# Packing the small matmuls of an RWKV-7 recurrence into parts of the TensorE array, and starting the first two tiles from half-tile loads

## The reference, cut to what matters

```
h = rms_norm(x, norm_mix);  p = h @ w_in            # 512 x 2048 times 2048 x 9000-odd
q, k_att, v_att, rw, gate_a, gate_b = split_last(p, IN_SPLITS)
y_attn = sliding_window_attention(q, k_att, v_att, sinks)          # 16 heads of 64
def step(S, inp):                                    # RWKV-7, 16 heads of 64, 512 steps
    r_t, w_t, k_t, v_t, kk_t, a_t = inp
    sa = einsum('bhij,bhj->bhi', S, -kk_t)
    S = S * w_t + sa x (kk_t * a_t) + v_t x k_t
    return S, einsum('bhij,bhj->bhi', S, r_t)
merged = sigmoid(gate_a) * (y_attn @ w_branch_attn) + sigmoid(gate_b) * (y_rwkv @ w_branch_rwkv)
x = x + merged @ w_out
x = x + (silu(h2 @ ffn_gate) * (h2 @ ffn_up)) @ ffn_down;  out = rms_norm(x, norm_final)
```

## Time and profile before

| | |
|---|---|
| median of three runs | 3014.94 us |
| the profiled execution | 3015.46 us |
| its span, first to last instruction | 3013.4 us |
| mean granted TensorE clock | 0.994 of full speed |
| PE busy | 2949.5 us, 98% of the span, 15226 instructions |
| DVE, ACT, POOL busy | 917.6, 946.9, 1291.0 us |
| first matmul begins | 11.74 us |
| HBM traffic | 98 GB/s mean |

### The profile page before, as it was taken

How to read it: one execution, slowest core, us unless ns; L and a number is a source line. 1 busy time by engine, 2 the same in 40 slices (tenths; PEclk the granted TensorE clock), 3 DMA queues, 4 the chain that set the end, 5 groups by cost and what they waited for, 6 DMA issues and landing times.

```text
span 3013.4 us, 38711 instructions
## 1 busy us (share of the span) xinstructions
PE 2949.5 (98%) x15226; PEld 2373.1 (79%) x15226; DVE 917.6 (30%) x1380; ACT 946.9 (31%) x1213; POOL 1291.0 (43%) x1037
## 2 busy tenths in 40 slices
PE   7999999999999998999999999999999999999997
PEld 5777777777777776788888888888888888888885
DVE  5566355264363453433331110111101111011123
ACT  4354333343343343222233321233213331122221
POOL 5333324233233233555554444444445444544453
PEclk9999999999999999999999999999999999999998
DMA  4212212122122123343433222322222222322222
GB/s 160 84 71 97 77 60 101 59 78 86 54 81 90 50 97 115 133 146 140 146 139 139 97 82 98 113 97 96 83 100 98 97 97 86 109 97 97 89 88 102
DMA packets 63225, 296.12 MB, mean 98 GB/s; under 512 B 6688, under 2 KB 7968, under 8 KB 38688
## 3 DMA queue, kind: packets, MB, share of 16 engines
q1 hardware_dynamic: 55168, 280.17, 26.3%
q10 hardware_dynamic: 7968, 14.68, 1.3%
HBM read 274.12 MB, written 20.71 MB: 98 GB/s over the span
## 4 chain that ended last, share of the span: by engine, by line
PE 92%; DVE 3%; issue 2%; ACT 1%; POOL 1%; DVEq 0%; DMA 0%; POOLq 0%; SPq 0%; ACTq 0%
PE dense L1181 27%; PE dense L1183 26%; PE dense L1182 26%; PE work L1384 1%; PE work L1365 1%; PE work L1182 1%; PE work L1181 1%; PE work L1183 1%; PE work L1374 1%; DVE Y L1022 1%; PE work L1341 1%; POOL wlo L474 1%; PE work L1353 0%; PE work L1434 0%; PE work L1342 0%
## 5 line engine op out<-in xcount | busy, mean ns | idle before, releaser
L474 POOL TENSOR_TENSOR wlo<-raw,whi 128x512 fp32r<-128x512 f32 (+1 forms) x1016 | 1265.9, 1276 | 1684.8 <-ACT whi L520 1684.8
L1181 PE MATMUL dense<-H_hi,whi 128*128 128x512 f32 x2672 | 1080.1, 404 | 26.8 <-DVE wlo L806 11.7
L1183 PE MATMUL dense<-H_hi,wlo 128*128 128x512 f32 x2672 | 1044.7, 391 | 0.0
L1182 PE MATMUL dense<-H_lo,whi 128*128 128x512 f32 x2672 | 1043.5, 391 | 0.0
L520 ACT ACTIVATE whi<-raw 128x2048 fp32r<-128x2048 f32 (+1 forms) x255 | 454.6, 1783 | 1474.0 <-PE dense L1183 1394.1
L1181 PEld LDWEIGHTS dense<-H_hi,whi 128*128 128x128 f32 x2672 | 502.9, 188 | 162.5 <-issue 39.3
L1183 PEld LDWEIGHTS dense<-H_hi,wlo 128*128 128x128 f32 x2672 | 502.9, 188 | 108.4
L1182 PEld LDWEIGHTS dense<-H_lo,whi 128*128 128x128 f32 x2672 | 503.7, 189 | 101.2 <-issue 5.8
L1183 PE MATMUL dense<-G_hi,wlo 128*128 128x512 f32 x704 | 273.9, 389 | 0.0
L1181 PE MATMUL dense<-G_hi,whi 128*128 128x512 f32 x704 | 273.9, 389 | 0.0
L1182 PE MATMUL dense<-G_lo,whi 128*128 128x512 f32 x704 | 273.9, 389 | 0.0
(11 more groups left out here) (235 smaller groups left out, 2365.8 us busy)
## 6 DMA issues: line engine op xcount, KB each, us to landing
raw<-w_slots SPq DMA_DIRECT2D x103, 1024.0 KB, 4.9
raw<-w_gu SPq DMA_DIRECT2D x88, 1024.0 KB, 4.7
raw<-w_down SPq DMA_DIRECT2D x64, 704.0 KB, 4.0
gates_dram<-gout ACTq DMA_DIRECT2D x32, 256.0 KB, 2.0
gin<-gates_dram SPq DMA_DIRECT2D x16, 512.0 KB, 3.9
X<-xT SPq DMA_DIRECT2D x8, 512.0 KB, 10.5
xin<-xT SPq DMA_DIRECT2D x16, 256.0 KB, 3.5
x_dram<-x ACTq DMA_DIRECT2D x16, 256.0 KB, 3.7
```

The costliest lines, as they stand in the source:

```text
L474: done = nc.gpsimd.tensor_tensor(wlo[s][:, at], raw[s][:, at], whi[s][:, at].bitcast(f32), SUB)
L1181: PE.matmul(bank[:], whi[s][:, wk], hi[:, k, :], start=(k == first), stop=False)
L1182: PE.matmul(bank[:], whi[s][:, wk], lo[:, k, :], start=False, stop=False)
L1183: done = PE.matmul(bank[:], wlo[s][:, wk], hi[:, k, :], start=False, stop=(k == last))
```

## The change

It has two parts.

**Packing in the recurrence.** (a) The second product of each level is cut finer: for each head and block, instead of one matmul with 64 rows and 128 columns of weights on 64 moving columns, there are two with 64x64 weights on 32 moving columns, so that the four of a block lie in the four quadrants of the array (row part e, column part c). The last level has the same form now. (b) The first join writes head e to the partitions of `heads[e]`, so its matmuls alternate between column parts; its results then lie in both halves of `Lt`, ScalarE copies them in one operation of 128x256 and the transposes in two of 64x256. (c) The second join takes its weights from row part e and writes to bank `RP[e]`, so its matmuls alternate between row parts, and VectorE copies it in two operations. (d) The Gram blocks are issued as `icl` for both heads and then `kap` for both, and the wait for the banks comes once for each t.

**The start.** The first halves of weight tiles 0 and 1 are loaded right behind the first and the second X transfer, the second halves behind the fourth and the sixth. ScalarE splits the two tiles in quarters of 512 columns between the `H_hi` parts, and the squares come behind all of them; its table is loaded ahead by a small copy. VectorE does all low parts of tiles 0, 1 and 2 and the whole sum of squares. GpSimd begins with tile 3. TensorE takes four steps of tile 0, four of tile 1, and so on for two quarters, then the rest of tile 0 and the rest of tile 1; the sum over the squares comes behind tile 2. `kT` and `vT` move to memory that X held.

The diff, cut to its core:

```
@@ loads (SyncE)
             for g in range(KD // 2):
-                if g == 1:
-                    load(index(0, 2, 0))
-                    load(index(0, 2, 1))
                 sp.dma_start(X[:, 2 * g:2 * g + 2, :], ...).then_inc(x_loaded[g], 16)
+                if g < 2:
+                    sp.dma_start(raw[g][:, 0:half], w_slots[g][:, 0:half]).then_inc(first_raw[g], 16)
+                if g in (3, 5):
+                    s = (g - 3) // 2
+                    sp.dma_start(raw[s][:, half:SLOT], ...).then_inc(raw_loaded[s], 16)
@@ GpSimd
-            pool.wait_ge(lo_ready, 1)
-            low_part(index(0, 2, 1))
...
-            low_part(index(0, 2, 2))
+            pool.wait_ge(lo_ready, 3)
@@ ScalarE
+            act.wait_ge(warm, 1)
+            copy(tmp1[:, 0:1], proj[:, 0:1])
+            for q in range(4):
+                first_split(0, q)
+                for k in range(4 * q, 4 * q + 4):
+                    hi_part(k)
+                if q < 2:
+                    first_split(1, q)
+            for q in (2, 3):
+                first_split(1, q)
+            for k in range(6):
                 square(k)
+            split(index(0, 2, 2))
             act.wait_ge(tile_done, 1)
             copy(kT[0][:], dense[0][:]).then_inc(evacuated, 1)
-            split(index(0, 2, 2))
+            for k in range(6, KD):
+                square(k)
+            split(index(0, 2, 3))
@@ ScalarE, joins
-                    copy(join_w, R[4][0:CHUNK, :]).then_inc(join_w_read, 1)
+                    copy(join_w, R[4][:, 0:NB * CHUNK]).then_inc(join_w_read, 1)
-                    copy(join_x, R[3][0:CHUNK, :]).then_inc(join_x_read, 1)
+                    for e in range(2):
+                        done = copy(join_x[heads[e]], R[3][0:CHUNK, e * NB * CHUNK:(e + 1) * NB * CHUNK])
@@ TensorE, start
+            for q in range(4):
+                first_steps(0, q)
+                if q < 2:
+                    first_steps(1, q)
+            for q in (2, 3):
+                first_steps(1, q)
+            front_tile(index(0, 2, 2))
             pe.wait_ge(cst_loaded, 16)
-            for j in range(2):
-                pe.wait_ge(sq_used[j], KD // 2)
-                done = PE.matmul(R[0][:], ones, sqsum[j][:], start=(j == 0), stop=(j == 1))
+            pe.wait_ge(sq_used, KD)
+            PE.matmul(R[0][:], ones, sqsum[:], start=True, stop=True).then_inc(ss_done, 1)
@@ TensorE, Gram blocks
-                            if w >= 4:
-                                pe.wait_ge(l_read, p * (2 * NB) + w - 3)
+                        if t >= 2:
+                            pe.wait_ge(l_read, p * (2 * NB) + 2 * t - 2)
@@ TensorE, second product of a level
+                                for c in range(2):
+                                    first_col = t * HALF + c * (HALF // 2)
+                                    done = PE.matmul(RP[e][heads[c], first_col:first_col + HALF // 2],
+                                                     Xc[heads[e], t, heads[c]],
+                                                     W1[heads[e], t, c * (HALF // 2):(c + 1) * (HALF // 2)],
@@ TensorE, joins
+                            done = PE.matmul(R[4][heads[e], at], Lcross[second, e, t, :],
                                              Y[second, e, t, second], start=True, stop=True)
...
+                            done = PE.matmul(RP[e][first, at], join_x[heads[e], at],
+                                             join_w[heads[e], at], start=True, stop=True)
```

More of the change, by code:

```diff
@@ L54 @@
 DSLOT = FG * P
+QUARTER = SLOT // 4
 LOW_PIECES = 4
@@ L157, in build_layer @@
     att = Arena(nc, start.at)
+    kT = [att(f"kT{g}", [T_SEQ]) for g in range(STAGES)]
+    vT = [att(f"vT{g}", [T_SEQ]) for g in range(STAGES)]
     pT = att("pT", [2, 2, T_SEQ])
@@ L191, in build_layer @@
     Xc = Lt[:, 0]
[L192 to L193 removed]
+    join_x, join_w = (Lt[:, i].rearrange("p t n -> p (t n)")[:, 0:NB * CHUNK] for i in range(2))
     W1 = rw("W1", [NB, HALF])
@@ L236, in build_layer @@
         hi_ready, lo_ready = sem("hi_ready"), sem("lo_ready")
+        first_raw = [sem(f"first_raw{s}") for s in range(2)]
+        first_hi, first_lo, warm = sem("first_hi"), sem("first_lo"), sem("warm")
         tile_done = sem("tile_done")
@@ L558, in _ @@
             A.activation(rstd1[:], rstd1[:], ACT.Sqrt).then_inc(rms_ready, 1)
-            for n in range(1, ATT_TILES):
+            for n in range(2, ATT_TILES):
                 split(index(0, 2, n + 2))
@@ L793, in fence @@
                 V.drain()
-            V.memset(proj[:, 0:1], 0.0)
+            V.memset(proj[:, 0:1], 0.0).then_inc(warm, 1)
             dve.wait_ge(norms_loaded, 16)
[L799 to L812, removed]
+            V.memset(sqsum[:], 0.0)
@@ new lines, in _ @@
+            for q in range(4):
+                first_low(0, q)
+                for k in range(4 * q, 4 * q + 4):
+                    dve.wait_ge(h_hi_ready, k + 1)
+                    V.scalar_tensor_tensor(H_lo[:, k, :], X[:, k, :], norm_g[:, 0, k:k + 1],
+                                           H_hi[:, k, :].bitcast(f32), MUL, SUB).then_inc(h_lo_ready, 1)
+                if q < 2:
+                    first_low(1, q)
+            for q in (2, 3):
+                first_low(1, q)
+            for k in range(6):
+                add_square(k)
@@ L814, in _ @@
+            dve.wait_ge(hi_ready, 3)
+            V.tensor_tensor(wlo[0][:], raw[0][:], whi[0][:].bitcast(f32), SUB).then_inc(lo_ready, 1)
+            for k in range(6, KD):
+                add_square(k)
             dve.wait_ge(ss_done, 1)
@@ L1400, in _ @@
                     first, second = heads
[L1401 to L1404, removed]
+                    for t in range(NB):
+                        at = slice(t * CHUNK, (t + 1) * CHUNK)
+                        for e in range(2):
+                            done = PE.matmul(R[4][heads[e], at], Lcross[second, e, t, :],
                                              Y[second, e, t, second], start=True, stop=True)
```

112 lines of the change are left out of this document (54 added, 58 removed).

## The result

The changed kernel takes 2988.03 us (median of four runs, 2986.98 to 2988.91), against 3014.80 before; the ratio is 0.9911, with a 95% interval of 0.9899 to 0.9922. The forecast was 2986.5, with 2979 to 3001 around it. The profiled execution took 2988.91 us, its span is 2987.1, 26.3 less than before.

A forecast was written before the change was run, and what follows sets the result against it. The prediction took PE, busy 92%, as the bound: 13.5 us from the start plus 15.0 from eight pairs of the recurrence make 28.5, so 3015.46 becomes 2987.0, or 2986.5 by the median; range 2979 to 3001.

The forecast's parts named there:

- first matmul: At the kernel's start, PE's first matmul was to come at 8.4 us instead of waiting until 11.74.
- lost to the half-speed clock: At the start, PE running at half clock was to cost 2.0 us, within 1.4 to 3.0.
- tile 3 begins: PE was to reach weight tile 3 at 44.4 us instead of 57.9, gaining 13.5, bounds 10 and 15.
- levels, a pair: Second product in quadrants: burst 0.69 us instead of 1.11, three levels saving 0.42 and the last 0.11, 1.37 per pair.
- Gram wait, a pair: Waiting for two Gram blocks delays DVE's fifth: 0.42 us lost; a rival at 0.10 had no cost, 2983 us.
- joins, a pair: The recurrence's two joins were to shorten from 1.11 to 0.69 and 1.14 to 0.64, saving 0.42 and 0.50 us.
- all of a pair: Sum for one pair of the recurrence: 1.37 + 0.42 + 0.50 - 0.42 = 1.87 us; times 8, 15.0.
- The level that the prediction struck: Level where a gate tile ends: PE arrives 0.4 us earlier but waits for ACT, so its saving was not counted.
- From there on nothing of it is given back: After tile 3 begins, the start's 13.5 us was to be kept: a tile takes PE 11 us, GpSimd 5.
- the two-wide quadrants: Rival, chance 0.15: quadrants of the second product overlap in two rows only, a pair's levels give -0.27 us, total 2999.6.
- the slower one at 59 ns an instruction: Rival, chance 0.03: quadrant instructions don't overlap, 32 take 2.1 us instead of 1.11, total 3039 us.
- the weak start: Rival, chance 0.12: DVE or ACT falls behind, PE stutters, the clock falls; the start gains 6 to 8, total 2993.

The follow-up runs named there:

- experiment 10: Changed kernel with the second product of the levels back in its old form, all else as changed: 3000.57 us, ratio 0.9952.
- experiment 3: Changed kernel with the Gram blocks in the old order and with the old waits, one block read ahead of each: 2985.39 us, ratio 0.9904.
- experiment 1: The new start alone, with the recurrence as in the kernel before: 3004.30 us, ratio 0.9965.
- experiment 4: Changed kernel with ScalarE's sigmoid and store of a gate tile three steps into the next tile, split unmoved: 2984.19 us, ratio 0.9899.
- experiment 5: Changed kernel with GpSimd's low part of tile 14 held until VectorE has normalised one attention unit's probabilities: 2986.94 us, ratio 0.9906.
- experiment 2: The packed recurrence alone, with the start of the kernel before: 2999.83 us, ratio 0.9948.
- experiment 6: Changed kernel with a level's second product issued for all blocks of head 0, then all of head 1: 2990.82 us, ratio 0.9920.
- experiment 9: Kernel of experiment 7 with one dense step per pair moved from before the token transposes to the end of level 0: 2975.30 us, ratio 0.9868.
- experiment 7: Changed kernel with the edits of experiment 3, experiment 4 and experiment 5 together: 2979.19 us, ratio 0.9880.
- experiment 8: Kernel of experiment 7 with the second product also issued head by head, as in experiment 6: 2982.06 us, ratio 0.9893.

## Why the prediction was right

| term | forecast, us | measured, us |
|---|---|---|
| first matmul | 8.4 | 8.98 |
| lost to the half-speed clock | 2.0 | 2.6 (13 matmuls of 0.43 instead of 0.23) |
| tile 3 begins | 44.4 | 44.95; 57.9 before |
| given back in attention | 0 | 1.3 near 194; 0.8 near 218, not in every kernel |
| levels, a pair | 1.37 | 1.44 (experiment 10) |
| Gram wait, a pair | -0.42 | -0.43 (experiment 3) |
| joins, a pair | 0.92 | 0.43 + 0.46 by the bursts, in no experiment of their own |
| all of a pair | 1.87 | 1.85 (the three rows above give 1.90) |
| behind the last pair | 0 | 0.8 less |
| all, by the profiled spans | 28.5 | 26.3 |

**The start.** The mechanism was as forecast: no wait ahead of tiles 1, 2 and 3. The first matmul is late because ACT doesn't get the first half tile at 6.2 but at 6.8: the prediction took 400 GB/s for it, and from 5.0 to 6.25 us the transfers moved half of that. Why, no run shows; experiment 1 has a like dip (229 and 180). The clock stayed at half for 5.5 us instead of the 4 that I took, within its bounds. ACT's split of tile 3 ended at 38.9 instead of 37.8, GpSimd took 5.91 us for its four blocks, with VectorE's last additions beside it, and the margin ahead of tile 3, which I gave as 0.5 to 1.4, is 0.06. That nothing waited there was close.

**The levels.** Two prices stood against each other: the row of 28 instructions in 0.44 us, and the estimate of 1.0 us for the burst by the rule of some 60 cycles for each matmul (the Trainium skill, TensorEngine Tiling (Array Packing), Instruction Overhead). The trace doesn't agree with the rule here: 32 instructions take 0.67, 14 ns from start to start. Experiment 10 shows that all of the burst's gain counts in the levels that don't wait for ScalarE: three of 0.44 and the forecast 0.11 of the last are 1.43, and 1.44 is measured. The level that the prediction struck was struck rightly: in experiment 4 it is this wait that goes, and a pair gains 0.43.

**The Gram blocks.** The loss stood in the rows of before: VectorE without a gap is the bound, so a block that comes to it later costs that time. Experiment 3 shows it.

**What was wrong** is the sentence "From there on nothing of it is given back". It looked only at whether a tile's low part is in time for PE. Pulling the start forward by 13 us also moved GpSimd's work against VectorE's within a unit of attention, and experiment 5 shows that this costs some 1.1 to 1.4 us. The second wait cost another 0.8.

**What was luck.** By the profiled spans 26.3 us were gained: 12.9 at the start, less 2.1 in attention, 14.8 in the pairs, and 0.8 behind the last pair, for which the forecast had no term. Behind it PE stands idle for some 7.5 us and goes on at half speed. That stretch, before and after (as the earlier trace rows):

```profile
1195.60:1205.84 10.24, 6.21 (x15) 0.50 0.82 291
...
1171.65:1178.48 6.83, 4.38 (x10) 0.50 0.76 276
```

The rest of the kernel behind the last variance matmul takes 1822.4 us before and 1821.5 after. In the seven kernels where this stretch is 10.2 us long (before, experiments 1, 2, 3, 5, 6 and 9) it takes 1821.7 to 1822.4, and in the four where it is 6.8 (the changed kernel, experiments 4, 7 and 8) 1821.1 to 1821.5. (Experiment 10 has two such stretches, 6.8 and 3.4, and takes 1822.7.) Kernels with all of the change have either length (experiments 5 and 6, and 4 and 7), so the 0.8 isn't shown to be the change's own, and the forecast had no reason to hold it. Without it the total would stand further from the forecast.

None of the rivals came: not the two-wide quadrants, not the slower one at 59 ns an instruction, not the weak start; and the Gram wait did cost.

## What to carry to other kernels

Look in the trace for a burst with the form that yours is to have, the same columns of weights and the same parts of the array, and price yours by that row: in rounds, one instruction in each part, not by the number of instructions. Before waits are merged into one, see which engine is the bound there; if it is the one that reads the results, a first result that comes later costs its whole delay. A gain on PE ends where another engine's program order has something long ahead of a short copy. An earlier start moves every meeting of VectorE with GpSimd behind it: look for the rows in which a small VectorE operation takes several times its usual length.

## What the runs showed of the hardware

- A part of the array started its next float32 instruction after 111 ns with 128 columns of weights (the levels' old second product), after 58 ns with 64 columns and after 32 ns with 32 columns (the last level's old product). With 64 columns it was 58 ns whether 64 columns moved (the joins) or 32 (the new second product). So in these bursts the pace went by the columns of the weights, and what the quadrants saved is that the weights have 64 columns instead of 128.
- Four 64x64 quadrants took instructions with 32 moving columns at 14 ns from start to start in alternating order, and at 23 ns on average (0.70 us for 31 distances) when all of one row part came first. In that order the first instruction of the other row part, 17th as issued, started ahead of six that were issued before it.
- A VectorE pass of 128x256 lasted 0.35 us alone (four in 1.14) and 1.37 when it started behind one of GpSimd's subtractions (four in 4.20, of which three did).
- The second wait of attention came in two lengths: 1.2 us in eight of the twelve profiled kernels, and 2.0 to 2.1 in four (the changed kernel, experiments 2, 5 and 6). The eight have VectorE's `sinkexp` at 0.15 us and the four at 1.32 to 1.33, and in all twelve a GpSimd subtraction starts within 0.03 us behind it. What decides whether VectorE is held up by it stays open.
